# SwiGLU of each expert in two halves with the down units behind them, outputs copied by two engines, and a final norm spread over four engines

## The reference, cut to what matters

```
logits = h @ w_router + b_router;  top 4 of 32 experts, gates = softmax over the 4
gu   = xb @ w1[e] + b1[e]                       # 1024 -> 2048
gate = minimum(gu[:, :1024], 7);  up = clip(gu[:, 1024:], -7, 7)
y    = ((up + 1) * gate * sigmoid(1.702 * gate)) @ w2[e] + b2[e]   # 1024 -> 1024
x    = x + sum over the chosen experts of gate_weight * y
out  = x * rsqrt(mean(x*x) + 1e-5) * g_final
```

## Time and profile before

| | us |
|---|---|
| median of 3 runs (lowest to highest) | 1241.31 (1238.46 to 1241.55) |
| the profiled execution's own time | 1241.03 |
| its span on the core | 1239.2 |
| PE busy, PEld busy | 1167.4, 630.5 |
| DVE, ACT, POOL busy | 282.8, 166.1, 31.9 |
| DMA, gate/up weights, issue to landing (median) | 24.3 |
| DMA, down weights, issue to landing (median) | 20.3 |
| bytes moved | 458.60 MB, mean 370 GB/s |

### The profile page before, as it was taken

One profiled execution on the slowest core, in us unless ns is written; L12 is line 12 of the kernel. 1 busy time (PEld: TensorE's weight loads), 2 busy tenths in 40 slices (PEclk: granted clock), 3 DMA queues, 4 the chain that ended last, 5 costly groups with the idle time before them and its releaser, 6 DMA issues.

```text
span 1239.2 us, 15028 instructions
## 1 busy us (share of the span) xinstructions
PE 1167.4 (94%) x6004; PEld 630.5 (51%) x6004; DVE 282.8 (23%) x609; ACT 166.1 (13%) x267; POOL 31.9 (3%) x69
## 2 busy tenths in 40 slices
PE   8999999999999999899999999989999899999995
PEld 7888887774444444344444434433444343334443
DVE  5114532342111111112211111111111111111115
ACT  2011011021111111111111112111111111111112
POOL 1000000010000000000000000000000000000000
PEclk9999999999999999999999999999999999999998
DMA  9953334946999999999999999999999999999991
GB/s 374 406 177 136 128 146 167 427 191 245 415 427 428 426 428 428 426 426 430 426 428 427 426 430 425 427 428 427 427 429 428 425 429 427 428 427 427 428 394 55
DMA packets 37837, 458.60 MB, mean 370 GB/s; under 512 B 5744, under 2 KB 5744, under 8 KB 7056
## 3 DMA queue, kind: packets, MB, share of 16 engines
q1 hardware_dynamic: 35424, 454.11, 87.4%
q10 hardware_dynamic: 2352, 3.54, 0.8%
HBM read 454.41 MB, written 3.23 MB: 369 GB/s over the span
## 4 chain that ended last, share of the span: by engine, by line
DMA 50%; PE 45%; DVE 3%; issue 1%; SPq 0%; ACT 0%; DVEq 0%; ACTq 0%
DMA ring<-in_w_gu 50%; PE ps L1149 16%; PE ps L925 15%; PE ps L1196 5%; PE ps L943 2%; PE ps L1104 1%; PE ps L1124 1%; PE ps L1179 1%; DVE arena L851 1%; DMA ring<-in_w_k 1%; PE ps L1011 1%; PE ps L1042 1%; PE ps L1051 1%; PE ps L1021 1%; DVE arena L863 0%
## 5 line engine op out<-in xcount | busy, mean ns | idle before, releaser
L1149 PE MATMUL ps<-ring,arena 128*64 128x512 f32 x2048 | 457.3, 598 | 41.5 <-DMA ring<-in_w_gu 32.6
L1149 PEld LDWEIGHTS ps<-ring,arena 128*64 128x64 f32 x2048 | 144.3, 138 | 349.0 <-issue 278.6
L1196 PE MATMUL ps<-ring,arena 128*64 128x512 f32 x1024 | 226.8, 595 | 6.2 <-DVE arena L863 6.2
L830 DVE TENSOR_TENSOR resid<-resid,ps 128x264 f32<-128x264 f32 x128 | 51.3, 427 | 726.4 <-PE ps L1124 726.4
L925 PE MATMUL ps<-arena,ring 128*128 128x264 f32 (+1 forms) x832 | 186.6, 386 | 3.1 <-DMA ring<-in_w_k 1.7
L925 PEld LDWEIGHTS ps<-arena,ring 128*128 128x128 f32 x832 | 157.4, 190 | 30.6 <-DMA ring<-in_w_k 2.3
L1196 PEld LDWEIGHTS ps<-ring,arena 128*64 128x64 f32 x1024 | 70.7, 137 | 146.9 <-issue 130.7
L1104 PE MATMUL ps<-arena 128*128 128x128 f32 x816 | 102.6, 283 | 0.2 <-DVE arena L612 0.2
L1104 PEld LDWEIGHTS ps<-arena 128*128 128x128 f32 x816 | 100.0, 198 | 0.7 <-DVE arena L612 0.7
L545 ACT ACTIVATE arena<-ps 128x1024 f32<-128x1024 f32 x32 | 32.8, 1024 | 450.8 <-PE ps L1149 450.8
L1124 PE MATMUL ps<-arena 128*128 128x264 f32 x256 | 72.6, 396 | 0.0
(11 more groups left out here) (190 smaller groups left out, 423.2 us busy)
## 6 DMA issues: line engine op xcount, KB each, us to landing
ring<-in_w_gu SPq DMA_DIRECT2D x128, 2048.0 KB, 24.3
ring<-in_w_dn SPq DMA_DIRECT2D x64, 2048.0 KB, 20.3
ring<-in_w_in SPq DMA_DIRECT2D x10, 1024.0 KB, 27.6
ring<-in_kc SPq DMA_DIRECT2D x8, 1024.0 KB, 4.8
ring<-in_vc SPq DMA_DIRECT2D x8, 1024.0 KB, 4.8
ring<-in_w_v SPq DMA_DIRECT2D x4, 1024.0 KB, 24.0
ring<-in_w_out SPq DMA_DIRECT2D x4, 1024.0 KB, 5.8
ring<-in_w_q SPq DMA_DIRECT2D x4, 1024.0 KB, 4.7
```

Source lines behind the costliest of these rows:

```text
L830: TTN(resid[:, m, :], resid[:, m, :], ps[:, 6 + m % 2, 0:T], ALU.add).then_inc(c_added, 1)
L1149: last = mm(ps[64 * h:64 * h + 64, n, :], xg[:, cur, k, SLOTS * (j % 2):SLOTS * (j % 2) + SLOTS], w[:, at:at + 512], start=(k == 0), stop= ...
L1196: last = mm(ps[64 * h:64 * h + 64, 4, :], hid[:, k, :], w[:, at:at + 512], start=(k == 0), stop=(k == KT - 1))
```

## The change

- ACT copies only bank 0 to the left half of `gu_sb`; DVE copies bank 1 to the right half. The eight transposes become four after the left copy and four after the right one, each with its own `t_done`.
- Bias, clip, sigmoid and product work on four of the eight tiles at a time; `hid_ready` counts halves. Down unit 4 waits for half 0 and unit 5 for half 1.
- Combines 2 and 3 stand between down unit 4 and down unit 5. The gather is cut in two: parts 0 and 1 stand between gate/up unit 0 and unit 1, parts 2 and 3 behind combine 1. The `w_hot` transposes stand at the head of the expert, ahead of the gate/up matmuls.
- After `d_done` ACT copies the left half of y, DVE the right half.
- At the end the table for the root is loaded ahead of the squares. GpSimd adds the squares of tiles 0 to 3; TensorE sums that and the tiles 4 to 7 in PSUM with five matmuls. DVE scales tiles 0 to 4; tiles 5 to 7 get the gain from ACT and the factor from GpSimd, and ACT stores them in one DMA of 396 KB. SP stores the others in three.

```
         @block.gpsimd
+            for m in range(1, 4):
+                pool.wait_ge(sq_ready, 20 + m)
+                if m > 1:
+                    pool.wait_ge(late_sum, m - 1)
+                nc.gpsimd.tensor_tensor(ssum[:, 0:T], h_fm[:, 0, :] if m == 1 else ssum[:, 0:T], h_fm[:, m, :],
+                                        ALU.add).then_inc(late_sum, 1)
+            pool.wait_ge(rstd_ready, 5)
+            for m in range(5, KT):
+                pool.wait_ge(y_scaled, m - 4)
+                nc.gpsimd.tensor_tensor(resid[:, m, :], resid[:, m, :], rstd[:, 0, :], ALU.mult).then_inc(y_pool, 1)
...
         @block.scalar
-                    act.wait_ge(gu_done, e + 1)
-                    act.wait_ge(t_done, e + 1)
-                    nc.scalar.activation(gu_sb.rearrange("p (a b) -> p a b", a=2), ps[:, 0:2, :],
-                                         ACT.Copy).then_inc(gu_copied, 1)
...
-                    act.wait_ge(g_ready, e + 1)
-                    nc.scalar.activation(sig[:], tb[:, :, 0:SLOTS], ACT.Sigmoid, scale=ALPHA).then_inc(sig_ready, 1)
+                    act.wait_ge(gu_done, e + 1)
+                    act.wait_ge(t_done, e * 2 + 1)
+                    nc.scalar.activation(gu_sb[:, 0:512], ps[:, 0, :], ACT.Copy).then_inc(left_copied, 1)
+                    for h in range(2):
+                        act.wait_ge(g_ready, e * 2 + 1 + h)
+                        nc.scalar.activation(sig[:, 4 * h:4 * h + 4, :], tb[:, 4 * h:4 * h + 4, 0:SLOTS], ACT.Sigmoid,
+                                             scale=ALPHA).then_inc(sig_ready, 1)
...
-                    nc.scalar.activation(y_hot[row:row + 64, i // 2, 0:512], ps[0:64, 4, :], ACT.Copy)
-                    nc.scalar.activation(y_hot[row:row + 64, i // 2, 512:1024], ps[64:128, 4, :],
-                                         ACT.Copy).then_inc(y_copied, 1)
+                    nc.scalar.activation(y_hot[row:row + 64, i // 2, 0:512], ps[0:64, 4, :], ACT.Copy).then_inc(y_left, 1)
+            nc.scalar.activation(warm[:], eps[:], ACT.Sqrt)
...
+            for m in range(5, KT):
+                nc.scalar.activation(resid[:, m, :], resid[:, m, :], ACT.Copy,
+                                     scale=par_of("g_final")[:, m:m + 1]).then_inc(y_scaled, 1)
+            act.wait_ge(y_pool, 3)
+            act.dma_start(y_t[:, 5:KT, :], resid[:, 5:KT, :]).then_inc(y_stored, 16)
...
         @block.vector
+                    dve.wait_ge(gu_done, e + 1)
+                    copy(gu_sb[:, 512:1024], ps[:, 1, :]).then_inc(right_copied, 1)
                     dve.wait_ge(c_added, e * 4 + 1)
-                    for r in range(2):
+                    combine(e * 4, 4 * (i % 2))
+                    for h in range(2):
+                        tiles = slice(4 * h, 4 * h + 4)
+                        dve.wait_ge(t_done, e * 2 + 2 + h)
...
+                        TTN(gate_v, turned[:, :, 0, :], bc(bias[:, 0, :], 2, [P, 4, SLOTS]), ALU.add).then_inc(t_read, 1)
...
+                        TTN(hid[:, tiles, :], up_v, sig[:, tiles, :], ALU.mult).then_inc(hid_ready, 1)
+                    for r in range(1, 4):
                         combine(e * 4 + r, 4 * (i % 2) + r)
...
+                    dve.wait_ge(d_done, e + 1)
+                    row = SLOTS * (i % 2)
+                    copy(y_hot[row:row + 64, i // 2, 512:1024], ps[64:128, 4, :]).then_inc(y_right, 1)
             dve.wait_ge(c_added, end * 32 + 1)
             for m in range(KT):
                 dve.wait_ge(c_filled, end * 32 + m + 1)
                 TTN(resid[:, m, :], resid[:, m, :], ps[:, (0, 1, 2, 3, 5, 6, 7, 4)[m], 0:T], ALU.add).then_inc(c_added, 1)
-                if m:
-                    add_squares(h_fm, m - 1, 20)
-            add_squares(h_fm, KT - 1, 20)
...
-            for m in range(KT):
+            for m in range(5):
                 STT(resid[:, m, :], resid[:, m, :], par_of("g_final")[:, m:m + 1], rstd[:, 0, :],
...
         @block.tensor
+                    pe.wait_ge(left_copied, e + 1)
+                    pe.wait_ge(right_copied, e + 1)
                     for u in range(4):
+                        if u == 1:
+                            pe.wait_ge(side_copied, pos + 1)
+                            pe.wait_ge(p_built, twin + 2)
+                            gather(ps[:, 5, :], j % 2, (0, 1))
                         w = expert_unit(u)
...
+                    combine(e * 4, 0, 4 * (i % 2), pair, biased)
+
+                    pe.wait_ge(t_read, e * 4 + 1)
+                    for h in range(2):
+                        pe.wait_ge(right_copied if h else left_copied, e + 2)
+                        for f in range(4):
+                            last = turn(ps[:, 2 + h, P * f:P * f + P],
+                                        gu_sb[:, 512 * h + f:512 * h + f + ROWS_DN * (P - 1) + 1:ROWS_DN], ident[:])
+                        last.then_inc(t_done, 1)
+
+                    combine(e * 4, 1, 4 * (i % 2) + 1, pair, biased)
+                    gather(ps[:, 5, :], j % 2, (2, 3)).then_inc(side_filled, 1)
+
+                    pe.wait_ge(y_left, e + 1)
+                    pe.wait_ge(y_right, e + 1)
                     for u in range(4, UNITS):
+                        if u == 5:
+                            for r in range(2, 4):
+                                combine(e * 4, r, 4 * (i % 2) + r, pair, biased)
+                        pe.wait_ge(hid_ready, e * 2 + u - 3)
                         w = expert_unit(u)
...
-            pe.wait_ge(sum_ready, 5)
-            mm(ps[:, 0, 0:T], ones[:], ssum[:, 0:T], start=True, stop=True).then_inc(final_ssq, 1)
+            pe.wait_ge(c_added, end * 32 + 1 + 1)
+            pe.wait_ge(late_sum, 3)
+            mm(ps[:, 0, 0:T], ones[:], ssum[:, 0:T], start=True, stop=False)
+            for m in range(4, KT):
+                pe.wait_ge(sq_ready, 20 + m)
+                last = mm(ps[:, 0, 0:T], ones[:], h_fm[:, m, :], start=False, stop=(m == KT - 1))
+            last.then_inc(final_ssq, 1)
```

103 lines of the change are left out of this document (41 added, 62 removed).

## The result

The changed kernel takes 1245.03 us (median of 7 runs, 1243.15 to 1245.97), the kernel before 1240.74 us on the same chip (7 runs, 1238.46 to 1243.04). The ratio is 1.0034 with a 95% interval of 1.0022 to 1.0045: 0.34% slower, small but clear of the scatter, where 0.3% faster was forecast. The profiled execution took 1245.03 us, its span is 1243.2 us, 4.0 us longer than before.

The account below looks back on a forecast made before the run. The weight DMA stream was taken to bound the loop at 29.36 us an expert; 0.2 us at the stream's start plus 3.9 in the tail made 4.1, from 1241.03 to 1236.9 us, own range 1235.8 to 1238.0, 8-in-10 range 1234.4 to 1240.2.

Parts of the forecast that it names:

- Against 29.36 nothing of it is seen: Expert loop: TensorE's 27.4 to 27.9 us an expert stays hidden behind the weight stream's 29.36 us.
- cost nothing here: Expert loop: two-engine gate/up and y copies and the extra waits are free while half a gather's 1.5 us covers them.
- Rival 3: Each expert's wait for `hid` half 0 before down unit 4: TensorE becomes the bound, 1252 us; chance 0.05.
- The tail: Last expert's end of gate/up to the span's end: 4.8 us earlier last DMA, less 0.9 for the store, gains 3.9.
- The hand-off: Last expert, gate/up to down: unit 4 starts at 1211.5 instead of 1213.67; moved combines take back 1.0 of 2.2 us.
- the y copies: After the last down matmul: split over two engines, 0.9 us until the combines instead of 1.47, gaining 0.6.
- The squares: End combines to end of the sum: 6.8 us instead of 8.7, gaining 1.8, with GpSimd adds of 0.626 us.
- The scaling: First scaling to end of span: 5.5 us instead of 5.8, five DVE scalings at 0.41 each beside GpSimd's three.
- Rival 1: Final scaling: VectorE and GpSimd exclude each other, 1.1 us lost net, 3.0 gained overall, 1238.0 us; chance 0.22.
- The start of the stream: Second expert's first weight units: issued 0.5 to 1.1 us later, 1.1 regained; 0.2 us gained net.
- dry queue: Second expert, between landings of units 3 and 4: late use of unit 4 left the stream empty 1.1 us, which goes.
- TensorE's cycle: TensorE's time per expert in the loop: shorter by some 1 us, from 28.3 to 28.8 down to 27.4 to 27.9.

Follow-up runs that it names:

- the short loop: The changed kernel with VectorE's loop written for four experts per iteration instead of eight, twice the iterations: 1239.80 us, ratio to the kernel before 1.0000.
- both mends: The changed kernel with VectorE's loop of four experts and all eight scalings on VectorE: 1239.25 us, ratio to the kernel before 0.9990.

## Why the prediction was wrong

- **The step that failed: "Against 29.36 nothing of it is seen", and the copies and waits "cost nothing here".** The loop was charged as executed work only; as such it does stay hidden, as the short loop shows. What was left out is that 95 more instructions in the loop have to be brought in. That moved the last landing by 6.2 us in the profiled execution, 5.2 of them felt; by the ratios of the changed kernel with and without the short loop it is 0.34%, 4.2 us. In the profiled execution the span's forecast was missed by 4.1 + 4.0 = 8.1 us: 6.2 are this, 1.9 the tail, 1.1 the stream's start, less the 1.0 by which the landing stands further into the tail (8.2, the rest is rounding). The page of before had the hint: it lists two instruction queues, and the plateau of the earlier trace rows was read only as bytes a second.
- **Rival 3** had the sign and not the mechanism. TensorE did not become the bound, though it came nearer to it than forecast: down unit 4, which waits for `hid` half 0, began 4.2 us behind the end of gate/up, as forecast, and at least three units stood in the queue all along. The gaps appear in the kernel before too, when fills are added to it.
- **The tail: 3.9 forecast, 2.0 measured.** The hand-off held to the tenth. Down and combines took 0.2 more, the y copies 0.2 more. The squares took 7.3 instead of 6.8: GpSimd's adds take 0.74 and start 0.89 apart, where 0.626 and 0.08 between were counted; the matmuls of the sum ran at the forecast pace, five in 2.5. The scaling lost 0.6 where 0.3 were to be gained.
- **Rival 1, the exclusion, was true,** and its 1.1 us net loss was 0.9 (6.4 for 5.5). VectorE and GpSimd together need 3.55 us; by the prediction's 0.7 and 0.41 a piece one after the other would be 4.2, side by side 2.1. That lies between, but the 0.7 was a guess, and a product without VectorE beside it was never measured. The single durations say more: as long as GpSimd works, each scaling starts 0.89 us behind the last instead of 0.41, at GpSimd's own pace, so the two take turns. The rule that the prediction weighed (the Trainium skill, "SBUF — State Buffer", "Who interferes with whom") calls the shared ports an exclusive lock, and lets a VectorE instruction with two SBUF inputs contend with a GpSimd one that reads SBUF. The trace agrees that such instructions are hit here, and that the adds which read PSUM are not: 3.47 / 8 = 0.43 each, with GpSimd's sum of squares beside them.
- **The start of the stream: 0.2 gained was forecast, and it seems to be lost.** The first landing came 0.8 early, but unit 4 was still late (issued 309.7 - 289.6 = 20.1 us behind unit 0, where 19.6 was the limit) and the excess until 330 us rose from 1.1 to 2.8. By the landing of the third expert's first unit, the four kernels with the changed loop are at 330.4 to 331.7, mean 330.9, the eight with the old one at 327.0 to 331.1, mean 329.4. These are single executions, and the ranges overlap; if the 1.5 us hold, they are most of what the 2.0 us of the tail bring, and explain why the changed kernel with the short loop is level with before. That wasn't tested by itself. Nor does the prediction's reading of the 1.1 us as a dry queue hold up: in the eight kernels with the old loop unit 4 was issued 20.5 to 20.6 us behind unit 0 each time, but landed 4.98 to 6.77 us behind unit 3. Two q14 fetches fall between 299 and 311 us in all of them; whether they make these gaps stays open.
- **TensorE's cycle** was to shrink by 1 us and grew by 1.0, from 27.2 to 28.2, and here the mechanism was wrong. From the end of gate/up to the first down matmul it saves 6.4 - 4.2 = 2.2 us. But before, the gather and the combines stood in just this stretch and cost nothing, since TensorE waited there for VectorE's SwiGLU anyway (0.25 us were left to wait). Now half of the gather (1.61) lengthens gate/up, from 13.73 to 15.67, and two combines (1.09) lengthen down, from 7.09 to 8.32. For the last expert the prediction counted the combines in this way (the 1.0 taken back of 2.2), for the loop it counted neither. It had no price, as the stream was slower still.

With both mends the changed kernel gains 0.1%, if that. The shorter tail is real and small; the cost lay where no instruction was slow.

## What to carry to other kernels

Where a kernel runs at the rate of its weight stream, unrolled loop code is traffic of the same DMA engines: before lengthening an engine's loop body, look at the page's instruction queues, and prefer fewer experts per iteration to a body that no longer stays resident. A gap between landings while several units are queued can't be the consumers' fault; look for what else the DMA engines carried in that gap. An edit that moves instructions to an idle engine is cheap in time, but its code has a length. And work that fills a wait is free only where it stands: moved elsewhere, it lengthens the cycle.

## What the runs showed of the hardware

- VectorE's loops of up to 248 instructions (waits not counted) ran without a fetch in the later iterations; at 271, 272 and 368 there were five fetches of 8 KB in each.
- Such a fetch takes about 1 us off a stream at 428 GB/s, though its 8 KB are 0.02 us of it. With 6 of them from 525 us on the excess is 6.5, as with none; with 12 or 13 it is 11.8 to 13.2 in all, 0.96 to 1.02 a fetch, in place of the 6.4 and not on top of them. In the packets it is one of the unit's sixteen records that slips.
- The 16 KB fetches of q8, a little more than one an expert, go with the 6.4 us of excess that every kernel here has; a gap of 1.2 to 1.5 us follows about every eighth. Without them the stream would be 0.5% shorter, an estimate from the 6.4 us that holds only if the picture does.
- Closing a loop that isn't resident held VectorE up 5.2 to 7.0 us, in the shadow of the stream; a resident loop's edge took 0.7 us at most.
- In one execution TensorE's clock was granted at 0.57 over 3.7 us, shortly after an idle of 2.33 us near the stream's end, which made 16 matmuls 1.7 us longer.
- GpSimd's products and VectorE's scalings, both with two 128x264 inputs in SBUF, take turns: one of each every 0.89 us, where scalings alone follow each other every 0.41.
